# Memory attention with queries, keys, probabilities and values as high and low parts

## The reference, cut to what matters

```python
def memory_cross_attention(h, mem_n, w_mem_q, w_mem_kv, w_mem_o):
    q = jnp.einsum("bsd,de->bse", h, w_mem_q).reshape(B, S, MEM_HEADS, MEM_HEAD_DIM)
    kv = jnp.einsum("bmd,de->bme", mem_n, w_mem_kv)
    ...
    s = jnp.einsum("bshd,bmhd->bhsm", q, k).astype(jnp.float32) * (MEM_HEAD_DIM ** -0.5)
    p = jax.nn.softmax(s, axis=-1).astype(v.dtype)
    o = jnp.einsum("bhsm,bmhd->bshd", p, v).reshape(B, S, D_MODEL)
    return jnp.einsum("bse,ed->bsd", o, w_mem_o)
```

## Time and profile before

| | us |
|---|---|
| median of three runs | 1484.63 |
| lowest and highest run | 1484.05, 1487.74 |
| profiled execution, own time | 1484.37 |
| its span in the trace | 1482.6 |
| PE busy in the span | 1440.1 (97%) |
| DVE busy in the span | 851.4 (57%) |
| ACT busy in the span | 552.9 (37%) |
| POOL busy in the span | 990.2 (67%) |
| memory attention, first score product to first product of `mem_o` | 31.1 |

### The profile page before, as it was taken

One profiled execution on the slowest core, in us unless ns is written; L12 is line 12 of the kernel. 1 busy time (PEld: TensorE's weight loads), 2 busy tenths in 40 slices (PEclk: granted clock), 3 DMA queues, 4 the chain that ended last, 5 costly groups with the idle time before them and its releaser, 6 DMA issues.

```text
span 1482.6 us, 18612 instructions
## 1 busy us (share of the span) xinstructions
PE 1440.1 (97%) x6987; PEld 1169.7 (79%) x6987; DVE 851.4 (57%) x1334; ACT 552.9 (37%) x1075; POOL 990.2 (67%) x400
## 2 busy tenths in 40 slices
PE   3999999999999999999999999999999999999997
PEld 3888877778898888888898844789789888888886
DVE  6998156554565555666744786441516555465655
ACT  3201133433454344444333376452424523333214
POOL 1857554355668899888568996365153989788653
PEclk9999999999999999999999999999999999999999
DMA  9875321223543332322443200133024323232131
GB/s 349 298 270 209 100 85 57 86 86 106 169 153 114 114 113 87 114 86 85 156 126 109 86 1 1 59 125 123 7 86 142 114 86 114 86 114 86 57 97 74
DMA packets 103385, 167.88 MB, mean 113 GB/s; under 512 B 3917, under 2 KB 61185, under 8 KB 102785
## 3 DMA queue, kind: packets, MB, share of 16 engines
q1 hardware_dynamic: 100176, 160.45, 31.7%
q10 hardware_dynamic: 3121, 6.26, 1.4%
HBM read 161.97 MB, written 4.72 MB: 112 GB/s over the span
## 4 chain that ended last, share of the span: by engine, by line
PE 84%; DVE 10%; ACT 3%; DMA 2%; issue 1%; POOL 1%; DVEq 0%; SPq 0%; ACTq 0%; POOLq 0%
PE bank L911 25%; PE bank L913 25%; PE bank L912 25%; DVE bank L2054 2%; DMA ada_w<-in_w_ada 1%; DVE smx L2507 1%; DVE x L2050 1%; PE bank L1372 1%; PE bank L1429 1%; PE bank L1448 1%; DVE bank L2050 1%; PE bank L1183 1%; DVE m L2050 1%; ACT junk L1541 1%; PE bank L1195 1%
## 5 line engine op out<-in xcount | busy, mean ns | idle before, releaser
L911 PE MATMUL bank<-ht_hi,w_hi 128*128 128x512 f32 (+1 forms) x1200 | 442.9, 369 | 0.5 <-DVE ht_lo L2050 0.3
L912 PE MATMUL bank<-ht_hi,w_lo 128*128 128x512 f32 (+1 forms) x1200 | 440.1, 367 | 0.0
L913 PE MATMUL bank<-ht_lo,w_hi 128*128 128x512 f32 (+1 forms) x1200 | 440.0, 367 | 0.0
L759 POOL TENSOR_TENSOR w_lo<-w_raw,w_hi 128x2048 fp32r<-128x2048 f32 x83 | 389.8, 4697 | 6.9
L757 POOL TENSOR_SCALAR w_hi<-w_raw 128x2048 fp32r<-128x2048 f32 x83 | 162.3, 1955 | 343.5 <-DMA w_raw<-in_w_in 111.2
L911 PEld LDWEIGHTS bank<-ht_hi,w_hi 128*128 128x128 f32 x1200 | 226.5, 189 | 41.6 <-issue 2.7
L913 PEld LDWEIGHTS bank<-ht_lo,w_hi 128*128 128x128 f32 x1200 | 226.6, 189 | 37.1
L912 PEld LDWEIGHTS bank<-ht_hi,w_lo 128*128 128x128 f32 x1200 | 226.6, 189 | 36.8 <-issue 0.5
L809 POOL TENSOR_TENSOR dn_lo<-dn_raw,dn_hi_all 128x1024 fp32r<-128x1024 f32 x77 | 184.6, 2418 | 56.7 <-ACT dn_hi_all L1738 56.6
L2054 DVE SCALAR_TENSOR_TENSOR uc<-bank,par,uc 128x511 f32<-128x511 f32 x88 | 66.0, 750 | 128.7 <-ACT uc L1992 125.6
L823 POOL TENSOR_TENSOR dn_raw<-dn_raw 128x1024 f32<-128x1024 f32 x44 | 105.8, 2404 | 12.8 <-PE bank L913 4.8
(11 more groups left out here) (305 smaller groups left out, 2415.7 us busy)
## 6 DMA issues: line engine op xcount, KB each, us to landing
w_raw<-in_w_in SPq DMA_DIRECT2D x27, 1024.0 KB, 5.0
ada_w<-in_w_ada SPq DMA_DIRECT2D x48, 512.0 KB, 7.3
w_raw<-in_w_up SPq DMA_DIRECT2D x22, 1024.0 KB, 5.0
w_raw<-in_w_mlp_in SPq DMA_DIRECT2D x16, 1024.0 KB, 5.5
dn_raw<-in_w_mlp_out SPq DMA_DIRECT2D x28, 512.0 KB, 4.8
w_raw<-in_w_out SPq DMA_DIRECT2D x8, 1024.0 KB, 5.0
w_raw<-in_w_mem_kv SPq DMA_DIRECT2D x8, 1024.0 KB, 5.2
dn_raw<-in_w_down SPq DMA_DIRECT2D x16, 512.0 KB, 4.7
```

Source lines behind the costliest of these rows:

```text
L759: g.tensor_tensor(w_lo[:, r], w_raw[:, r], w_hi[:, r].bitcast(F32), ALU.subtract).then_inc(slab_split, 1)
L911: inc_free(pe.matmul(o, ah, bh, start=start, stop=False))
L912: pe.matmul(o, al, bh, start=False, stop=False)
L913: return pe.matmul(o, ah, bl, start=False, stop=stop)
```

## The change

All four operands of the two plain products are split, and both products become `mm3`.

- ACT copies `mem_k` and `mem_v` once, rounded, into the room of `mt_lo` and `mt_hi`. POOL then subtracts these from the originals (`kv_lo`), ahead of the four slabs of `mem_o` in its queue. PE waits for both.
- ACT's eight copies of the queries become rounded copies `qm_hi`, and no longer free the banks. DVE makes `qm_lo` of each and frees the bank.
- ACT's copies of turned probabilities become rounded copies and no longer free the banks. DVE makes `ptm_lo`, at the t steps of the list, and frees the banks.
- PE issues 24 products of 256 columns for each z instead of 16 records, and 12 of 512 columns for each o instead of 8 records.

```diff
+        mem_k_hi = mt_lo
+        mem_v_hi = mt_hi[:].rearrange("p (a b) n -> p a (b n)", a=MT)
...
-            split_all(n, S0["ffn"] + 2)
+            split_all(n, S0["mem_o"])
+            g.wait_ge(kv_hi, 1)
+            g.tensor_tensor(mem_k_lo[:], mem_k[:], mem_k_hi[:].bitcast(F32), ALU.subtract).then_inc(kv_lo, 1)
+            g.wait_ge(kv_hi, 2)
+            g.tensor_tensor(mem_v_lo[:], mem_v[:], mem_v_hi.bitcast(F32), ALU.subtract).then_inc(kv_lo, 1)
+            split_all(S0["mem_o"], S0["ffn"] + 2)
...
-                        ins = pe.matmul(t.ap[:, 0:NM], qm[:, 2 * h + c, qt * P:qt * P + P], mem_k[:, 2 * h + c, :],
-                                        start=c == 0, stop=c == 1)
+                        q = slice(qt * P, qt * P + P)
+                        ins = mm3(t.ap[:, 0:NM], qm_hi[:, 2 * h + c, q], qm_lo[:, 2 * h + c, q],
+                                  mem_k_hi[:, 2 * h + c, :], mem_k_lo[:, 2 * h + c, :], c == 0, c == 1)
...
-                        ins = pe.matmul(t.ap[:], mem_v[:, kc, h * MHD + c * P:h * MHD + c * P + P], ptm_of[h % 2][:, kc],
-                                        start=kc == 0, stop=kc == MT - 1)
+                        d = slice(h * MHD + c * P, h * MHD + c * P + P)
+                        ins = mm3(t.ap[:], mem_v_hi[:, kc, d], mem_v_lo[:, kc, d], ptm_of[h % 2][:, kc],
+                                  ptm_lo[h % 2][:, kc], kc == 0, kc == MT - 1)
...
-            pe.wait_ge(k_back, 16)
+            pe.wait_ge(kv_lo, 2)
...
-                            st.done(act.copy(pt[h % 2][:, kc], t.ap[:]), tile=t)
+                            st.done(act.copy(pt[h % 2][:, kc], t.ap[:]), ptm_made)
...
+            act.wait_ge(k_back, 16)
+            st.after()
+            st.done(act.copy(mem_k_hi[:], mem_k[:]), kv_hi)
+            st.done(act.copy(mem_v_hi, mem_v[:]), kv_hi)
             for m in range(DC):
-                copy_out(T0["mem_q"] + m, qm[:, m])
+                t = Tile(T0["mem_q"] + m)
+                t.wait_full(act)
+                st.done(act.copy(qm_hi[:, m], t.ap[:]), qm_made)
...
+                    elif what == "t":
+                        for kc in range(MT):
+                            t = Tile(tiles["t", h] + kc)
+                            v.wait_ge(ptm_made, MT * h + kc + 1)
+                            tt(ptm_lo[h % 2][:, kc], t.ap[:], ptm_of[h % 2][:, kc].bitcast(F32), ALU.subtract, tile=t)
...
+            for m in range(DC):
+                v.wait_ge(qm_made, m + 1)
+                t = Tile(T0["mem_q"] + m)
+                tt(qm_lo[:, m], t.ap[:], qm_hi[:, m].bitcast(F32), ALU.subtract, tile=t)
```

More of the change, by code:

```diff
@@ L401, in build @@
             p1_sum = sb("p1_sum", [P, 2, T], where=lend)
-        mem_k = sb("mem_k", [P, DC, NM])
-        mem_v = sb("mem_v", [P, MT, D])
+        with ExitStack() as lend:
+            mem_k = sb("mem_k", [P, DC, NM], where=lend)
+            mem_v = sb("mem_v", [P, MT, D], where=lend)
+        mem_k_lo = sb("mem_k_lo", [P, DC, NM], F32R)
+        mem_v_lo = sb("mem_v_lo", [P, MT, D], F32R)
         mt_hi = sb("mt_hi", [P, DC, NM], F32R)
@@ L430, in build @@
         ph = ExitStack()
-        qm = sb("qm", [P, DC, T], where=ph)
+        qm_hi = sb("qm_hi", [P, DC, T], F32R, where=ph)
         pm = sb("pm", [P, 2, NT, NM], where=ph)
-        ptm = sb("ptm", [P, MT, T], where=ph)
+        ptm = sb("ptm", [P, MT, T], F32R, where=ph)
         gain5 = sb("gain5", [P, D], where=ph)
-        ptm_odd = sb("ptm_odd", [P, MT, T], where=ph)
+        ptm_odd = sb("ptm_odd", [P, MT, T], F32R, where=ph)
         ptm_of = (ptm, ptm_odd)
+        qm_lo = sb("qm_lo", [P, DC, T], F32R, where=ph)
+        ptm_lo = [sb(f"ptm_lo{i}", [P, MT, T], F32R, where=ph) for i in range(2)]
+        mem_k_hi = mt_lo
+        mem_v_hi = mt_hi[:].rearrange("p (a b) n -> p a (b n)", a=MT)
         ph.close()
@@ L471, in build @@
         squared, mlp_slab_hi, mlp_hi, mlp_sums = (sem(n) for n in ("squared", "mlp_slab_hi", "mlp_hi", "mlp_sums"))
+        qm_made, ptm_made, kv_hi, kv_lo = sem("qm_made"), sem("ptm_made"), sem("kv_hi"), sem("kv_lo")
         memory_kept, mt_back, k_back = sem("memory_kept"), sem("mt_back"), sem("k_back")
```

## The result

| | median of the runs, us | span of the profiled execution, us |
|---|---|---|
| before | 1485.25 (1484.05 to 1487.74, 6 runs) | 1482.6 |
| after | 1493.55 (1490.3 to 1494.01, 6 runs) | 1492.0 |

The ratio is 1.0051, interval 1.0038 to 1.0064. They need not be the quotient of the medians, since the runs of one kernel scatter over some 4 to 5 us.) The kernel is slower by more than the forecast, 1485.9, and outside the range that ended at 1488.8.

What follows compares the result with a forecast made beforehand. The prediction had DVE replace PE as the memory attention's bound: stage 0.6 us longer plus a 0.73 later start, +1.3 on 1484.37, so 1485.7, or 1485.9 as a median; range 1484.0 to 1488.8.

Steps and rivals of the forecast that it cites:

- Keys and values: Memory keys and values: ACT's copies (4.2 us) and POOL's two subtractions (4.6 each) are hidden, costing nothing.
- SP and slabs: Slab loading: z0's first `mm3` frees a slab, so `mem_o`'s third loads some 30 us earlier, worth nothing.
- PE's gain: Memory attention on PE: scores gain 2.3 us and values 2.9, work falling from 31.1 to 25.9 us.
- DVE takes over as bound, and PE waits at t3: Memory attention: DVE's chain sets a stage of 31.7 us, 0.6 longer; PE waits 2 to 3 us ahead of t3.
- Start of the stage, +0.73: Before the first score: DVE's subtraction of the last queries makes PE start 0.73 us later.
- Copies on ACT hidden: ACT's two rounded copies of keys and values, 2.1 us each, fit into 8.94 us of ACT's idle time.
- Hidden, with 22 us to spare: POOL's subtractions push `mem_o`'s first two slabs to about 1055; PE needs them at 1077, so no cost.
- Worth nothing: `mem_o`'s third slab, loaded some 30 us earlier, gains nothing, since it was split before PE reached it anyway.
- The clock at t3: Rival: PE's clock falls for a while at the gap before t3, costing +0.9 to +1.7 us; 16%.
- the two clock rivals: PE's clock falls at t3: briefly, 1486.8 to 1487.6 us, 16%; or to the end of the stage, 1491.3, 6%.
- the sum: Whole change: stage 0.6 us longer plus 0.73 later start, +1.3 us.
- The bounds of the sum: Whole change: shorter DVE subtractions take 0.7 off, hand-overs on ACT and PE add 1.6, giving +0.6 to +2.9 us.

Runs made afterwards that it cites:

- pool_head: `pool_scale` with PE waiting ahead of each head for that head's two blocks of queries instead of for all eight; 1483.51 us, ratio 0.9982.
- both edits: Changed kernel, POOL's key and value subtractions ahead of the last query slab, scores and values no longer signalling a free slab; 1487.12 us, ratio 1.0017.
- third slab late: Changed kernel with scores and values no longer signalling a free slab, so `mem_o`'s third slab is split only after `mem_o` begins; 1487.85 us, ratio 1.0023.
- pool_scale: The kernel with both edits, and its 16 scalings of the probabilities moved from DVE to POOL; 1484.06 us, ratio 0.9994.
- keys and values early: Changed kernel with POOL's two subtractions for keys and values moved ahead of the last slab of the queries; 1489.91 us, ratio 1.0032.

## Why the prediction was wrong, step by step

Two steps failed, the ones in *Keys and values* and in *SP and slabs* that priced POOL's work at nothing. The runs showed 6.49 us of DVE's time in their place. The prediction had given a loss of more than 0.3% a chance of 0.07; it is 0.51%.

- **PE's gain: right.** Scores start 0.120 apart and values 0.227, as predicted. PE's work in the stage isn't the bound. (It is busy 30.64 us there and not 26, for some 9 us at half the clock; in `pool_head`, at full clock, it is 26.69.)
- **DVE takes over as bound, and PE waits at t3: right, but mis-sized.** DVE is never idle from its first maximum to the low parts of t3, PE waits 2.46 there (2 to 3 forecast). One term was short: a pair of low parts is listed as 1.49, but the next instruction starts 1.58 or 1.59 behind its start (1078.26, 1079.84, 1081.43 for the last three). That is 0.1 for each of the five that others follow, 0.5 us, and small gaps add 0.15. Of the smaller waits forecast at t1, o0 and t2 the changed kernel shows none; with both edits there are 0.74 ahead of t1 and 0.35 ahead of o0.
- **Start of the stage, +0.73: right.** The subtraction of the last queries takes 0.69, and PE waits 1.70 for it instead of 1.01. The other 0.6 of the later start was already there upstream of the stage in this execution.
- **Copies on ACT hidden: right** (1.91 and 1.90 us, done at 1014.10; forecast 2.1 each).
- **"Hidden, with 22 us to spare", POOL's two subtractions: wrong.** They ran at 4.61 each, as said, and PE did get its slabs in time. But I asked only who waits for POOL's result, and not who can't work while POOL does. By the long scaling that is left with the third slab late, this step cost 0.66 us; taken out of the changed kernel it gave back 3.26 (6.49 to 3.23), since head 0's scalings were then done before the third slab's split began. The prices of the two steps depend on each other and don't add up. (The second slab was split by 1051.93; the prediction has both 1055 and 1052 for it.)
- **"Worth nothing", the early third slab: wrong.** It costs 1.70 + 4.13 us on DVE in the changed kernel, by the experiments most of the loss (1.0051 with it, 1.0023 without).
- **The clock at t3: the rival was right as a mechanism.** It fell for some 3.5 us and cost 0.6 us; its price had been 0.9 to 1.7. (In `pool_scale` it cost 1.5, last section.) At 6% and 16% the two clock rivals were asides to a loss that none of the rivals contained.

With POOL out of the way the sum nearly stands. From the last product of the queries to the first of `mem_o` the kernel before takes 32.52 us and the one with both edits 34.89, so 2.4 more where 1.3 was forecast, within the bounds of +0.6 to +2.9. The missing 1.1 is 0.7 on DVE's list (28.46 instead of 27.78) and 0.4 behind it (3.35 instead of 2.92). The prediction also held that differences within 0.3% can't be told from no change; with the runs made here the intervals are about 0.1% either way.

The bounds of the sum came from rows in which POOL is idle beside the scalings, and so could not contain the loss. The trace of before did have rows that show it, in another stage. A list by line, with the shortest, median and longest in ns of the four low parts that are made from SBUF to SBUF:

```profile
L2050 DVE TENSOR_TENSOR ht_lo<-ay,ht_hi x4: 692/692/4912, 947.4 to 954.0; 128x512 fp32r<-128x512 f32 x4
```

And the timelines of DVE and POOL there:

```profile
947.43 7.30 DVE L2050 TENSOR_TENSOR ht_lo<-ay,ht_hi 128x512 fp32r<-128x512 f32 x4
...
947.59 5.00 POOL L759 TENSOR_TENSOR w_lo<-w_raw,w_hi 128x2048 fp32r<-128x2048 f32 x1
```

Three of the four take 0.692 us and one takes 4.912, beside an instruction of POOL that itself takes 5.00 instead of 4.60. A longest instance seven times the median was the sign to look for.

The Trainium skill states the rule (page "SBUF — State Buffer", section "🔬 SBUF: two separate sides"): VectorE and GpSimd share one pair of SBUF ports; "The shared pair is an **exclusive lock**, not a bandwidth split", held for a whole instruction, and VectorE needs it in its modes with two ports, or with two inputs in SBUF against an instruction of GpSimd that reads SBUF. The page "Advanced Engine Details and Errata", section "Mode Summary", names source and destination in SBUF as a condition of a two-port mode. The traces agree for the forms seen here: the 128x256 scaling went from 0.35 to as much as 4.48 us, while maxima from PSUM (0.42) and one-column operations (0.15) were not held up. Read against the two steps above, that rule would have ruled them out.

## What to carry to other kernels

"Hidden" has two questions: who waits for the result, and which instructions of other engines can't run meanwhile. Before work is put on POOL, or made to run at another time (a semaphore signal that frees a buffer early is enough), list DVE's operations from SBUF to SBUF in that stretch, and look in the trace for such groups whose longest instance is far above the median. A stage where PE is 100% busy and DVE just keeps up with it gains little from faster matmuls if the split for them goes to DVE.

## What was not expected of the hardware

- An instruction of POOL holds up DVE's scaling in full (up to 4.13 us for one of 0.35), but not DVE's operations on PSUM or on single columns in the same microseconds.
- What PE's clock does behind a wait isn't told by the wait's length alone. With both edits, after 2.81 us of waiting ahead of t3, the clock was at the lower level at once, and so it was after 2.46 in the changed kernel and 2.20 with keys and values early. In the kernel with the late slab, after 2.79, the turn ran at full pace (1.09 us) and the clock fell some 1.9 us behind its start. In `pool_head`, after 2.28, it didn't fall in the stage; in `pool_scale`, after 2.28 too, it fell behind the turn. After the waits of 1.71 or less in the stage no fall followed in these kernels. Windows behind the wait ahead of t3, first with both edits:

```profile
1071.40:1073.00 1.60, 1.49 (x7) 1.49 (x8) 1.39 (x4) 0.72 (x2) 0.00 (x0) 0.50 0.00 0
```

With the third slab late, from the first product of o2 on:

```profile
1073.30:1076.00 2.70, 2.67 (x7) 2.13 (x8) 2.36 (x4) 0.48 (x2) 0.00 (x0) 0.59 0.00 0
```

And in `pool_head`:

```profile
1070.00:1072.00 2.00, 1.99 (x13) 1.82 (x14) 1.79 (x3) 1.36 (x3) 0.00 (x0) 1.00 0.00 0
```

What decides it was not tried. It is worth 1.5 us between `pool_scale` and `pool_head`: both have the same 25.19 us on DVE, and from DVE's last low part of t3 to the first product of `mem_o` PE needs 4.43 us in the first and 2.92 in the second. The prediction's terms for that stretch, 2.72 + 0.2, are just the 2.92 at full clock.
